# A diffusion layer on one core: the first phase's loads, sum of squares and modulation columns in another order

## The reference

```python
mod_ctx = (jax.nn.silu(c_ctx) @ w_ada[l] + b_ada[l])[None, :]
mod_lat = jax.nn.silu(c) @ w_ada[l] + b_ada[l]
...
shift1, scale1, gate1, shift2, scale2, gate2 = jnp.split(mod, N_MOD, axis=-1)
h = _modulate(_rmsnorm(x, p["norm1_g"]), shift1, scale1)
proj = h @ p["w_in"]
...
```

## Time and profile before

| | us |
|---|---|
| median of three runs | 1462.98 |
| the three runs | 1460.91 to 1463.7 |
| the profiled execution | 1459.86 |
| its span, first to last instruction | 1458.1 |
| PE busy in it | 1327.9 (91%) |
| DVE busy | 730.3 (50%) |
| ACT busy | 530.0 (36%) |
| mean granted clock of TensorE | 0.96 |

### The profile page before, as it was taken

How to read it: one execution, slowest core, us unless ns; L and a number is a source line. 1 busy time by engine, 2 the same in 40 slices (tenths; PEclk the granted TensorE clock), 3 DMA queues, 4 the chain that set the end, 5 groups by cost and what they waited for, 6 DMA issues and landing times.

```text
span 1458.1 us, 31772 instructions
## 1 busy us (share of the span) xinstructions
PE 1327.9 (91%) x13955; PEld 1222.8 (84%) x13955; DVE 730.3 (50%) x1085; ACT 530.0 (36%) x796; POOL 41.8 (3%) x84
## 2 busy tenths in 40 slices
PE   4799999997998799869993989989999999989996
PEld 2799999997997555569973968889999999989995
DVE  3517742734554389955544532165454545433534
ACT  3635534422334343313342211264343433333333
POOL 0000010000000000000001000000000000000000
PEclk9899999999999799989996999999999999999998
DMA  9222264313000200020006477211212211022222
GB/s 395 79 97 94 103 264 166 104 46 161 8 4 3 87 0 1 1 96 8 4 3 242 148 279 271 89 59 58 86 62 82 78 66 65 15 59 77 66 74 93
DMA packets 24761, 134.58 MB, mean 92 GB/s; under 512 B 2992, under 2 KB 3632, under 8 KB 16208
## 3 DMA queue, kind: packets, MB, share of 16 engines
q1 hardware_dynamic: 19088, 103.59, 19.9%
q0 software_dynamic: 5568, 29.40, 5.4%
HBM read 112.66 MB, written 20.32 MB: 91 GB/s over the span
## 4 chain that ended last, share of the span: by engine, by line
PE 83%; DVE 8%; ACT 3%; DMA 3%; issue 2%; PEld 1%; POOLq 0%; PEldq 0%; POOL 0%; SPq 0%; DVEq 0%; ACTq 0%
PE ps L675 45%; PE ps L1120 11%; PE ps L838 4%; PE ps L826 3%; PE ps L806 2%; PE ps L1025 2%; PE ps L710 1%; PE ps L984 1%; PE ps L818 1%; DMA xT<-in_x 1%; DVE rden L1802 1%; PE ps L700 1%; PE ps L1002 1%; DMA bld<-branch_scratch 1%; PE ps L949 1%
## 5 line engine op out<-in xcount | busy, mean ns | idle before, releaser
L675 PE MATMUL ps<-h2lo,whi 128*128 128x322 f32 x672 | 154.5, 311 | 0.7 <-ACT facc L1220 0.7
L675 PE MATMUL ps<-h2hi,wlo 128*128 128x322 f32 x672 | 155.0, 312 | 0.0
L675 PE MATMUL ps<-h2hi,whi 128*128 128x322 f32 x672 | 154.0, 310 | 0.0
L1512 DVE TENSOR_TENSOR wlo<-raw,whi 128x2048 fp32r<-128x2048 f32 x48 | 109.7, 2287 | 72.4 <-ACT whi L1182 72.4
L675 PE MATMUL ps<-hlo,whi 128*128 128x322 f32 x544 | 127.8, 316 | 1.0 <-ACT qkv L1246 1.0
L675 PE MATMUL ps<-hhi,wlo 128*128 128x322 f32 x544 | 125.4, 312 | 0.0
L675 PE MATMUL ps<-hhi,whi 128*128 128x322 f32 x544 | 124.7, 310 | 0.0
L675 PEld LDWEIGHTS ps<-h2hi,whi 128*128 128x128 f32 x672 | 114.2, 190 | 0.0
L675 PEld LDWEIGHTS ps<-h2lo,whi 128*128 128x128 f32 x672 | 113.0, 189 | 0.9 <-DVE wlo L1512 0.9
L675 PEld LDWEIGHTS ps<-h2hi,wlo 128*128 128x128 f32 x672 | 113.6, 189 | 0.0
L1556 DVE SCALAR_TENSOR_TENSOR facc<-fraw,par,facc 128x642 f32<-128x642 f32 x44 | 39.1, 888 | 139.2 <-ACT facc L1220 139.2
(11 more groups left out here) (312 smaller groups left out, 2636.9 us busy)
## 6 DMA issues: line engine op xcount, KB each, us to landing
raw<-in_wblk SPq DMA_DIRECT2D x48, 1024.0 KB, 4.9
adl<-in_wada SPq DMA_DIRECT2D x8, 2048.0 KB, 8.2
raw<-in_wdn SPq DMA_DIRECT2D x44, 256.0 KB, 2.6
adaw<-in_wada SPq DMA_DIRECT2D x4, 2048.0 KB, 17.5
gate_scratch<-gout POOLq DMA_DIRECT2D x16, 322.0 KB, 2.5
gld<-gate_scratch POOLq DMA_DIRECT2D x8, 644.0 KB, 4.1
attention_inputs_used<-attention_scratch SPq DMA_DIRECT2D x1, 5056.0 KB, 14.6
u_scratch<-uout POOLq DMA_DIRECT2D x12, 320.0 KB, 2.4
```

The source lines that it names most:

```text
L675: mm = pe.matmul(o, w, v, start=first, stop=last and w is hi and x is xh[n])
L1512: TT(wlo[s][:, :], raw[s][:, :], whi[s][:, :].bitcast(F32), ALU.subtract).then_inc(lo_done, 1)
```

## The change

In the first phase, SP loads par, then the first 130 columns of con (the identity and `sel`), then x, the four adaw blocks, the two raw blocks, and last the rest of con. The sum of squares is made of unsplit numbers: DVE adds the eight squares into rs one after another, and PE makes one plain fp32 sum over the partitions, after the first adaw block. ACT squares x ahead of all row copies. PE turns the rows of each block right after the next block's product. ACT splits the first weights before it waits for the columns, and DVE scales six blocks of x (buffers sqf and the four new xr4) ahead of the columns; the low half of the first weights then comes between. PE waits for the rest of con after the first projection block. The second use of `modulate` keeps two buffers.

```diff
--- before.py
+++ after.py
@@ -209,11 +209,10 @@
     wlo = [sb(f"wlo{s}", [P, WEL], F32R) for s in range(2)]
     after_ring = spot[0]
     sqf = [sb(f"sqf{s}", [P, TP]) for s in range(2)]
-    sqh = [sb(f"sqh{s}", [P, TP], F32R) for s in range(2)]
-    sql = [sb(f"sql{s}", [P, TP], F32R) for s in range(2)]
+    xr4 = [sb(f"xr{k}", [P, TP]) for k in range(4)]
     hf = [sb(f"hf{s}", [P, TP]) for s in range(2)]
     rs = sb("rs", [P, TP])
-    xr = sqf
+    xr = [sqf + xr4, sqf]
     norm_end = spot[0]
     hhi = [sb(f"hhi{k}", [P, TP], F32R) for k in range(KD)]
     hlo = [sb(f"hlo{k}", [P, TP], F32R) for k in range(KD)]
@@ -398,13 +397,13 @@
         return ap.rearrange("p (d q n) -> p d q n", d=2, q=n)
 
 
-    par_ld, con_ld, x_ld = sem("par_loaded"), sem("constants_loaded"), sem("x_loaded")
+    par_ld, con_ld, sel_ld, x_ld = sem("par_loaded"), sem("constants_loaded"), sem("selection_loaded"), sem("x_loaded")
     ada_ld = [sem(f"ada_loaded{s}") for s in range(ADA_EARLY)]
     w_ld = [sem(f"weights_loaded{s}") for s in range(2)]
     hi_done, lo_done = sem("weights_hi_split"), sem("weights_lo_split")
     tile_done, tile_evac = sem("product_tile_done"), sem("product_tile_read")
     conv_done = sem("convolved")
-    sq_done, sqs_done, sq_used, rs_done = sem("squares_ready"), sem("squares_split"), sem("squares_summed"), sem("rsqrt_ready")
+    sq_done, sqa_done, sq_used, rs_done = sem("squares_ready"), sem("squares_added"), sem("squares_summed"), sem("rsqrt_ready")
     hh_done = sem("modulated_hi")
     xr_done, hf_done, h_done = sem("normalized"), sem("modulated"), sem("modulated_split")
     ctanh_done, silu_done = sem("silu_tanh"), sem("silu_ready")
@@ -507,14 +506,14 @@
     @block.sync
     def _(sp):
         sp.dma_start(par[:, :], par_d).then_inc(par_ld, 16)
-        for n in range(2):
+        turn = CC["blk"]
+        sp.dma_start(con[:, 0:turn], con_d[:, 0:turn]).then_inc(sel_ld, 16)
+        sp.dma_start(xT[:, :, :], x_d).then_inc(x_ld, 16)
+        for n in range(ADA_EARLY):
             sp.dma_start(adaw[n][:, :, :], wada_d[n]).then_inc(ada_ld[n], 16)
-        sp.dma_start(xT[:, :, :], x_d).then_inc(x_ld, 16)
-        for n in range(2, ADA_EARLY):
-            sp.dma_start(adaw[n][:, :, :], wada_d[n]).then_inc(ada_ld[n], 16)
-        sp.dma_start(con[:, :], con_d).then_inc(con_ld, 16)
         for s in range(2):
             sp.dma_start(raw[s][:, :], wblk_d[s]).then_inc(w_ld[s], 16)
+        sp.dma_start(con[:, turn:], con_d[:, turn:]).then_inc(con_ld, 16)
         with sp.Fori(1, BLK_BR // 2) as i:
             for s in range(2):
                 sp.wait_ge(hi_done, 2 * i + s - 1)
@@ -654,16 +653,6 @@
 
     @block.tensor
     def _(pe):
-        def sum_squares(n):
-
-            outs = out_halves(4)
-            for k in range(KD):
-                pe.wait_ge(sqs_done, n * KD + k + 1)
-                for j, part in enumerate((sqh[k % 2], sql[k % 2])):
-                    for o, x in zip(outs, halves(part)):
-                        mm = pe.matmul(o, onesr[:, :], x, start=(k == 0 and j == 0), stop=(k == KD - 1 and j == 1))
-                mm.then_inc(sq_used, 1)
-
         def dense_tile(s, j, ks, xh, xl, outs, width, stop=True):
 
             for n, k in enumerate(ks):
@@ -731,18 +720,25 @@
             mm.then_inc(modt_done, 1)
 
 
+        def early_turn(n):
+            pe.wait_ge(row_done, n + 3)
+            for j in range(4 * n, 4 * n + 4):
+                mm = pe.matmul(bank(6, 2, 2 * j), modrow[:, j * P:j * P + P], sel, start=True, stop=True)
+            return mm
+
         pe.wait_ge(silu_done, 1)
+        pe.wait_ge(sel_ld, 16)
         for n in range(ADA_EARLY):
             ada_block(n, n % 2, adaw[n], (ada_ld[n], 16), 2)
-            if n == 1:
+            if n == 0:
                 pe.wait_ge(setup_done, 1)
-                sum_squares(0)
-        pe.wait_ge(row_done, ADA_EARLY + 2)
+                pe.wait_ge(sqa_done, KD - 1)
+                square_sum(rs, out_halves(4), True, True).then_inc(sq_used, KD)
+            else:
+                early_turn(n - 1)
+        early_turn(ADA_EARLY - 1).then_inc(modt_done, ADA_EARLY - 1)
+        dense_first(0, 0, hhi, hlo)
         pe.wait_ge(con_ld, 16)
-        for j in range(4 * ADA_EARLY):
-            mm = pe.matmul(bank(6, 2, 2 * j), modrow[:, j * P:j * P + P], sel, start=True, stop=True)
-        mm.then_inc(modt_done, ADA_EARLY - 1)
-        dense_first(0, 0, hhi, hlo)
         phase_over(pe, 1)
 
         def square_sums(i):
@@ -1142,12 +1138,13 @@
         st = Steps(ac, act)
 
         def x_squares():
+            ac.wait_ge(x_ld, 16)
             for k in range(KD):
-                if k == 0:
-                    ac.wait_ge(x_ld, 16)
                 if k >= 2:
-                    ac.wait_ge(sqs_done, k - 1)
+                    ac.wait_ge(sqa_done, max(1, k - 2))
                 ac.activation(sqf[k % 2][:, :], xT[:, k, :], ACT.Square).then_inc(sq_done, 1)
+
+        def x_rsqrt():
             ac.wait_ge(sq_used, KD)
             st.last(ac.activation(rs[:, :], tile(4), ACT.Ln, scale=1.0 / D, bias=EPS))
             ac.activation(rs[:, :], rs[:, :], ACT.Exp, scale=-0.5).then_inc(rs_done, 1)
@@ -1172,7 +1169,7 @@
                 if k >= 2:
                     ac.wait_ge(h_done, n * KD + k - 1)
                 for c, (a, w) in enumerate(((L0, LAT), (C0, CTX))):
-                    ins = ac.activation(hf[k % 2][:, a:a + w], xr[k % 2][:, a:a + w], ACT.Identity,
+                    ins = ac.activation(hf[k % 2][:, a:a + w], xr[n][k % len(xr[n])][:, a:a + w], ACT.Identity,
                                         scale=scale[:, k, c:c + 1], bias=modT[:, shift_at + k, c:c + 1])
                 ins.then_inc(hf_done, 1)
                 ac.wait_ge(hf_done, n * KD + k + 1)
@@ -1196,14 +1193,15 @@
             ac.wait_ge(ada_done, n + 1)
             ac.activation(modrow[:, n * 512:n * 512 + 512], bank(2 + n % 2), ACT.Copy).then_inc(row_done, 1)
 
+        x_squares()
         mod_row(0)
-        mod_row(1)
-        x_squares()
-        for n in range(2, ADA_EARLY):
+        x_rsqrt()
+        for n in range(1, ADA_EARLY):
             mod_row(n)
-        ac.wait_ge(mod_done, 1)
+        ac.wait_ge(ada_done, 2)
         ac.wait_ge(w_ld[0], 16)
         split_hi(0, 0)
+        ac.wait_ge(mod_done, 1)
         modulate(0, sc1g, 0, hhi)
         ac.wait_ge(w_ld[1], 16)
         split_hi(1, 1)
@@ -1487,25 +1485,26 @@
         st = Steps(dv, dve)
         TT, STT, TS = dv.tensor_tensor, dv.scalar_tensor_tensor, dv.tensor_scalar
 
-        def split_squares():
+        def added_squares():
+            for k in range(1, KD):
+                dv.wait_ge(sq_done, k + 1)
+                if k > 1:
+                    dv.wait_ge(sqa_done, k - 1)
+                TT(rs[:, :], (sqf[0] if k == 1 else rs)[:, :], sqf[k % 2][:, :], ALU.add).then_inc(sqa_done, 1)
+
+        def scaled(n, k, src):
+
+            TT(xr[n][k % len(xr[n])][:, :], src[:, k, :], rs[:, :], ALU.mult).then_inc(xr_done, 1)
+
+        def modulate(n, src, hi, lo, made):
+            ahead = len(xr[n])
+            for k in range(made, ahead):
+                scaled(n, k, src)
             for k in range(KD):
-                dv.wait_ge(sq_done, k + 1)
-                if k >= 2:
-                    dv.wait_ge(sq_used, k - 1)
-                st.last(dv.tensor_copy(sqh[k % 2][:, :], sqf[k % 2][:, :]))
-                TT(sql[k % 2][:, :], sqf[k % 2][:, :], sqh[k % 2][:, :].bitcast(F32), ALU.subtract).then_inc(sqs_done, 1)
-
-        def modulate(n, src, hi, lo):
-
-            dv.wait_ge(rs_done, n + 1)
-            for k in range(KD + 1):
-                if k < KD:
-                    if k >= 2:
-                        dv.wait_ge(hf_done, n * KD + k - 1)
-                    TT(xr[k % 2][:, :], src[:, k, :], rs[:, :], ALU.mult).then_inc(xr_done, 1)
-                if k:
-                    dv.wait_ge(hh_done, n * KD + k)
-                    TT(lo[k - 1][:, :], hf[(k - 1) % 2][:, :], hi[k - 1][:, :].bitcast(F32), ALU.subtract).then_inc(h_done, 1)
+                dv.wait_ge(hh_done, n * KD + k + 1)
+                TT(lo[k][:, :], hf[k % 2][:, :], hi[k][:, :].bitcast(F32), ALU.subtract).then_inc(h_done, 1)
+                if k + ahead < KD:
+                    scaled(n, k + ahead, src)
 
         def next_lo(b, s):
             dv.wait_ge(hi_done, b + 1)
@@ -1531,7 +1530,10 @@
         TS(qg8[:, :], pc("qg"), 0.125, None, ALU.mult)
         for s in range(2):
             dv.memset(hf[s][:, :], 0.0)
-        split_squares()
+        added_squares()
+        dv.wait_ge(rs_done, 1)
+        for k in range(len(xr[0])):
+            scaled(0, k, xT)
         def mod_columns(at, n, b, off=0):
 
             return TT(modT[:, at:at + n, :], bank(b, 2 * n, off).rearrange("p (k c) -> p k c", c=2),
@@ -1545,7 +1547,7 @@
         st.last(mod_columns(0, 16, 6))
         one_plus(sc1g, 8, "g1").then_inc(mod_done, 1)
         next_lo(0, 0)
-        modulate(0, xT, hhi, hlo)
```

(4 more changed lines are left out.)

## The result

The changed kernel takes 1448.47 us (1447.05 to 1448.89) where the kernel before takes 1463.04: a ratio of 0.9904, 95% interval 0.9888 to 0.9920. The forecast was 1452.3 and faster. Its profiled execution took 1448.89 us with a span of 1447.1, 11.0 us under the span in the earlier trace rows.

A forecast was written before the change was run, and what follows sets the result against it. TensorE's long chain waits for the first phase's end, so that end moves everything. Modulation's start moves from 47.16 to 36.2 (10.96), PE starts 0.25 later: gain 10.7, from 1462.98 to 1452.3 us; range 1447.5 to 1458.0.

The forecast's parts named there:

- Which chain decides: First phase: adaw loads cover the squares; last load, fourth product and turns, or first high split, decide when modulation starts.
- H: Moment ScalarE begins to modulate in the first phase: 47.16 us before, forecast 36.2, between 34.7 and 36.9.
- the meeting: End of the first phase, where all four engines meet: forecast at 55.65 us in place of 66.4.
- Loads: SP's load stream: x lands at 10.7 us in place of 20.3, the last adaw block at 30.2.
- Squares: Sum of squares from x: additions end at 19.0, sum takes 1.33 to twice that, all covered by adaw loads.
- Clock: TensorE's granted clock in the first phase: will fall and may come back; start of modulation two thirds towards 36.9.
- rival A: Clock warm throughout the first phase: modulation starts at 34.7, gain 12.1 us, time 1450.9; chance 0.20.
- the cold end: Half clock for fourth product (3.64 us) and turns (1.2 each): modulation starts at 36.9 us.
- rival D: Behind the first phase: clock falls at other moments; four or more extra falls cut gain under 2.9; about 1461; chance 0.05.
- Behind H: From modulation's start to the first phase's end: ScalarE/VectorE 19.17 us, PE starts 3.2 later and takes 16.25, ending last.
- rival B: Cold throughout, projection block 0 slow to warm, PE 0.6 to 1.2 later: gain 8.8 to 9.4, about 1453.9; chance 0.17.
- From there both traces run alike: Stages behind the first phase: unchanged, both traces staying 9 to 12 us apart; no gain counted there.

The follow-up runs named there:

- pad28: Changed kernel with 28 small extra products put ahead of PE's first product: 1450.09 us, ratio 0.9924 to the kernel before.
- before_pad50: Kernel before with 50 small extra products put ahead of PE's first product: 1459.22 us, ratio 0.9988 to the kernel before.
- before_again: Kernel before, unchanged, run once more for a second trace: 1461.81 us, ratio 1.0001.
- fill_pauses: Changed kernel with 28 small extra products in PE's pause ahead of the fourth adaw block and 50 behind the last turn: 1448.79 us, ratio 0.9917.
- later_and_fill: Changed kernel, constants' head loaded behind x and first adaw block; extra products: 34 at start, 12 before fourth block, 32 behind last turn: 1449.14 us.
- split_late: Changed kernel with the first high split of the weights put back behind the columns: 1449.64 us, ratio 0.9921 to the kernel before.
- x_after_adaw: Changed kernel with x loaded behind the four adaw blocks: 1464.80 us, ratio 1.0028 to the kernel before.

## Why the prediction came out right

- *Which chain decides.* Right: the last adaw load, the fourth product, two turns, then H; H + 3.06 for PE's start (forecast 3.2), PE last at the meeting (57.8), ScalarE and VectorE 0.8 us ahead (54.68 + 2.29 = 56.97).
- *Loads.* x at 11.7 and the last adaw block at 31.29 instead of 10.7 and 30.2. The step that failed was the price of the small load, taken by its bytes (0.16 us), with SP's issue put at nothing ("where nothing is late"). That issue stands ahead of x and moves it by 0.46 us; in all the small load in front cost some 0.5 us by the means, and 1.0 in this trace.
- *Squares.* Right in size: additions over at 20.3 (forecast x + 8.3; it was x + 8.6), the sum 2.27 (between 1.33 and twice that), rs at 25.5, and all of it covered.
- *Clock.* The fall came, and in the middle of the product: 2.51, between 1.92 and 3.64. In the eight traces with x early and nothing added in the pause, the fourth product took 1.92 (twice), 2.51, 2.60, 3.25, 3.39, 3.50 and 3.52: neither rival A nor the cold end is the rule. The term that was mis-sized is the turn at half clock: 1.2 us by the window of L743's records, 1.76 measured (16 records in 3.52). The window's 8 were all records that touch it; 6 begin in it. H was 37.81, past the "cold" end of 36.9 by 0.9: the load 1.1 later, the turns 1.1 longer, the product 1.1 shorter than at half clock, and 0.2 less for the drain and the two small operations.
- *The rivals' sums.* By the sum's own terms rival A gains 12.2 to 12.5 us, not 12.1, and rival D needs five more falls of 1.8 us, not four, to bring 10.7 under 2.9; neither matters for the result.
- *Behind H.* PE's block took 16.95 us instead of 16.25, since 5.0 us of it and not 3.6 were at half clock, within the 0.6 to 1.2 of rival B. Together: a meeting at 57.85, 8.5 us earlier, not 10.7.
- *Behind the meeting.* "From there both traces run alike" was wrong, though the instructions are the same: PE's code had become 28 matmuls shorter, and a pause in the recurrence went from 2.05 to 0.68 us and took a fall of the clock with it (pad28, before_pad50). This brings 2.1 us in that stretch (36.72 to 34.64) and made up for what the first phase fell short of; that it did was luck, since the sum had no term for it. It was in the trace of before, in a stage that the sum took as given.
- *The level.* The spans differ by 11.0, the medians by 14.6 us. The first trace of before was the better one of two: before_again has its copy at 68.49 and 1461.3 of span. From the means of two traces each (before 67.51 and 1392.19; after 57.67 and 1389.23) the copy gives 9.8 and the rest 3.0, 12.8 together, within what the ratio's interval allows. The number 1452.3 was near for the sum of two misses of opposite sign, not because each term held.

## What to carry to other kernels

When a prologue is bound by its loads, order them by the chain that needs the longest time after landing, and price what stays behind the last one: product, turns, splits. Prices at either clock must be measured for each kind of instruction (from begin to begin of its records, not from how many touch a window), a small load in front of a stream costs its issue as well as its bytes, and a fill of dummy work pays only if it can't overrun the load it waits beside. Before a gain of a few microseconds is put down to an edit, compare the stages that the edit doesn't touch, and add or remove idle instructions at the start: the length of the code alone can be worth as much.

## What the runs showed of the hardware that was not expected

- A pause of PE that moves through the code when matmuls are added or taken out ahead of it: always with 2245 matmuls ahead of it, 2.05, 1.76 and 2.05 us long (before, before_again, pad28), 0.67 to 0.85 us in the eight traces of the code that is 28 matmuls shorter, 0.57 us in before_pad50, whose code is 50 longer, none in fill_pauses and later_and_fill. It ends 2.2 to 2.4 us behind the begin of a 16384-byte instruction load.
- A product of 128x128 on the matrix of ones takes 0.116 us at full clock and 0.23 at half; the turns, two columns each, take 0.12 and 0.22 per record. So these two cost nearly the same, though one streams 64 times the columns of the other.
- The granted clock reads 1.00 during the first product of w_ada, before as after, while that product takes 3.64 us, as much as the fourth does at 0.52 in split_late (3.52). In x_after_adaw the column reads 1.00 again from 40.1 to 45.0, behind 25.7 us in which PE did nothing, while the sum takes 2.49 us instead of 1.33. In both places the duration tells the level, not the column.
